# The end of a diffusion layer's expert stage: where the last down weights are loaded, where the first result tiles get their roots, which engine adds two of them

## The reference

```python
def ec_moe(h, router_w, w_gate, w_up, w_down):
    ...
    gate, idx = lax.top_k(jnp.swapaxes(aff, 1, 2), cap)      # 128 of 1024 tokens for each expert
    xs = h[bidx, idx]
    hid = jax.nn.silu(jnp.einsum("becd,edf->becf", xs, w_gate)) * jnp.einsum("becd,edf->becf", xs, w_up)
    ye = jnp.einsum("becf,efd->becd", hid, w_down) * gate[..., None].astype(h.dtype)
    return jnp.zeros_like(h).at[bidx, idx].add(ye)
...
y_lat = ec_moe(h_lat, router_w[l], exp_w_gate[l], exp_w_up[l], exp_w_down[l])
x = x + mod_lat[5] * rms_norm(y_lat, norm_g[l, 3])
```

## Time and profile before

| what | us |
|---|---|
| device time, median of three runs (1355.75 to 1360.29) | 1359.91 |
| the profiled execution: span from its first to its last instruction | 1356.6 |
| TensorE busy in that span | 1233.9 |
| VectorE busy | 765.7 |
| ScalarE busy | 429.7 |
| GpSimd busy | 225.3 |

### The profile page before, as it was taken

How to read it: one execution, slowest core, us unless ns; L and a number is a source line. 1 busy time by engine, 2 the same in 40 slices (tenths; PEclk the granted TensorE clock), 3 DMA queues, 4 the chain that set the end, 5 groups by cost and what they waited for, 6 DMA issues and landing times.

```text
span 1356.6 us, 14715 instructions
## 1 busy us (share of the span) xinstructions
PE 1233.9 (91%) x5488; PEld 717.2 (53%) x5488; DVE 765.7 (56%) x1113; ACT 429.7 (32%) x1109; POOL 225.3 (17%) x204
## 2 busy tenths in 40 slices
PE   5999999999989999899999779991599999999992
PEld 3555555455445555689999534441344444444441
DVE  5299889887925888389898457647500101010106
ACT  6333242313111112578877335531011010101113
POOL 0300000010000021266667000000101111010112
PEclk9999999999999999899999989995699999999996
DMA  9923444552142433466766735527389999999967
GB/s 364 282 78 111 130 151 139 147 164 85 45 145 58 88 80 82 106 197 208 231 221 193 279 139 187 186 78 287 116 309 330 338 334 339 338 329 343 323 223 198
DMA packets 206164, 270.69 MB, mean 200 GB/s; under 512 B 73685, under 2 KB 122830, under 8 KB 206094
## 3 DMA queue, kind: packets, MB, share of 16 engines
q1 hardware_dynamic: 186182, 212.54, 48.0%
q0 software_dynamic: 13840, 50.86, 12.2%
q10 hardware_dynamic: 6072, 6.35, 1.4%
HBM read 217.75 MB, written 51.97 MB: 199 GB/s over the span
## 4 chain that ended last, share of the span: by engine, by line
PE 78%; DVE 11%; DMA 5%; SPq 2%; ACT 2%; issue 1%; POOLq 0%; ACTq 0%; DVEq 0%
PE ps L2007 23%; PE ps L1193 16%; PE ps L1216 8%; PE ps L1150 8%; PE ps L448 5%; PE ps L429 4%; DMA arena<-ada_w 2%; DVE arena L2445 2%; DVE arena L2374 2%; DVE arena L2443 2%; DMA arena<-w_in 1%; PE ps L1906 1%; PE ps L522 1%; PE ps L495 1%; DMA scan_dram<-arena 1%
## 5 line engine op out<-in xcount | busy, mean ns | idle before, releaser
L2007 PE MATMUL ps<-arena 128*128 128x512 f32 (+1 forms) x1072 | 425.2, 555 | 5.1 <-DMA arena<-w_in 5.1
L2007 PEld LDWEIGHTS ps<-arena 128*128 128x128 f32 x1072 | 202.2, 191 | 205.5 <-issue 195.2
L1193 PE MATMUL ps<-arena 128*128 128x512 f32 x512 | 226.9, 597 | 1.4 <-ACT arena L1338 1.4
L2374 DVE SCALAR_TENSOR_TENSOR arena<-arena,taps 128x1024 f32<-128x1024 f32 x160 | 207.3, 1296 | 5.5
L1193 PEld LDWEIGHTS ps<-arena 128*128 128x128 f32 x512 | 96.7, 192 | 116.6 <-issue 114.8
L1525 DVE TENSOR_TENSOR arena<-arena,ps 128x512 f32<-128x512 f32 x16 | 11.0, 687 | 223.2 <-PE ps L1193 223.2
L1150 PE MATMUL ps<-arena 128*128 128x512 f32 x256 | 116.7, 604 | 1.3 <-DMA arena<-w_out 1.3
L1216 PE MATMUL ps<-arena 128*128 128x512 f32 x256 | 112.5, 593 | 0.0
L448 PE MATMUL ps<-arena 128*128 128x128 f32 (+5 forms) x632 | 72.6, 261 | 6.8 <-DVE arena L658 3.9
L1216 PEld LDWEIGHTS ps<-arena 128*128 128x128 f32 x256 | 47.6, 191 | 54.0 <-issue 54.0
L1150 PEld LDWEIGHTS ps<-arena 128*128 128x128 f32 x256 | 47.4, 193 | 52.3 <-issue 50.8
(11 more groups left out here) (332 smaller groups left out, 1577.0 us busy)
## 6 DMA issues: line engine op xcount, KB each, us to landing
arena<-exp_w_gate SPq DMA_DIRECT2D x16, 2048.0 KB, 11.0
arena<-exp_w_up SPq DMA_DIRECT2D x16, 2048.0 KB, 9.7
arena<-exp_w_down SPq DMA_DIRECT2D x16, 2048.0 KB, 10.9
arena<-ada_w POOLq DMA_DIRECT2D x16, 1024.0 KB, 6.5
arena<-w_in SPq DMA_DIRECT2D x28, 512.0 KB, 4.9
arena<-ada_w SPq DMA_DIRECT2D x4, 2048.0 KB, 19.7
arena<-x SPq DMA_DIRECT2D x16, 512.0 KB, 6.4
arena<-g_dram SPq DMA_DIRECT2D x16, 512.0 KB, 5.6
```

The costliest lines, as they stand in the source:

```text
L1193: last = mm(ps[gu_bank[s] + j][:], xsT[s][:, k, :], ew[s][j][:, k, :], start=(k == 0), stop=(k == KD - 1))
L2007: last = mm(ps[3 * (m % 2) + gi][:, 0:w], wring[(m + 1) % NW][:, k, :], hT[:, k, o:o + w], start=(k == 0), stop=(k == KD - 1))
L2374: ins = v.scalar_tensor_tensor(accg, cin_l[ci % 2][:, j // 3:j // 3 + GR, j % 3:j % 3 + GW], tp[:, j:j + 1], accg, ALU.mult, ALU.add)
```

## The change

Six edits, all in the end. The numbers in brackets are lines of the changed kernel where they differ.

1. SP: `load_down` of expert 15 is no longer issued in the experts' loop, but behind the first four of the eight loads of `yt`, ahead of the other four.
2. ScalarE: the roots of tiles 0 and 1 stand ahead of the last `hidT` copy, those of tiles 2 and 3 ahead of expert 14's `ye` copy; the two row roots come last, behind those of all tiles. RANK is gone, since the roots now run in the order of their numbers.
3. N_ACC is 6: tiles 0 to 5 are stored with an addition by GpSimd's transfers, tiles 6 and 7 plainly.
4. For tiles 6 and 7 the addition of `x2` is GpSimd's (a `tensor_tensor` of 128x1024, then its own plain store), no longer VectorE's with a store by SP.
5. VectorE scales tiles 0 to 5 ahead of the addition of `ye` to expert 14's rows, then tiles 6 and 7, then finishes expert 14's rows (`row_done(0)`).
6. VectorE's work on expert 15's rows, from the down product on, comes behind all that, and `row_done(1)` is last.

```diff
--- before.py
+++ after.py
@@ -984,8 +984,7 @@
         assert NL * D == 2 * KD * F and EL % 2 == 0
         x2r, yr = (xs[EL % NX - 2], xs[EL % NX - 1]), (xs[EL % NX], xs[EL % NX + 1])
         assert NX == 4 and EL % NX == 2
-        N_ACC = 5
-        RANK = [0, 1, 2, 3, NL] + list(range(4, NL)) + [NL + 1]
+        N_ACC = 6
 
         wo_k = w_out.rearrange("a (k p) n -> (a p) k n", p=P)
         wg_e = exp_w_gate.rearrange("a e (k p) n -> (a e) p k n", p=P)
@@ -1065,16 +1064,14 @@
                     sp_.wait_ge(sem("y_zero"), 32 * NL)
                 if e + 1 < E_N:
                     load_in(e + 1)
-                load_down(e)
+                if e < E_N - 1:
+                    load_down(e)
             sp_.wait_ge(sem("y_sc"), 16 * EL)
             sp_.wait_ge(sem("gu"), 2 * EL + 2)
             for t in range(NL):
+                if t == NL // 2:
+                    load_down(E_N - 1)
                 sp_.dma_start(yt[:, t, :], y_t[t]).then_inc(sem(f"tile_in{t // 2}"), 16)
-            for i in range(LE):
-                sp_.wait_ge(sem(f"xs_in{i}"), 16 * (E_N // NX + 1))
-            for t in range(N_ACC, NL):
-                sp_.wait_ge(sem("fin"), t + 1)
-                sp_.dma_start(out_t[t], yt[:, t, :]).then_inc(sem("out_full"), 16)
             sp_.wait_ge(sem("out"), 16 * N_ACC)
             sp_.wait_ge(sem("out_full"), 16 * (NL - N_ACC))
             sp_.wait_ge(sem("out_rows"), 16 * LE)
@@ -1339,9 +1336,8 @@
 
             def root_of(i, src):
 
-                n = RANK.index(i)
                 a(sqj, src, ACT.Square, accum_out=ssq[:, i:i + 1]).then_inc(sem("ysq"), 1)
-                act.wait_ge(sem("ysq"), 2 * n + 1)
+                act.wait_ge(sem("ysq"), 2 * i + 1)
                 a(rstd[:, i:i + 1], ssq[:, i:i + 1], ACT.Sqrt, scale=1.0 / D, bias=eps1[:]).then_inc(sem("ysq"), 1)
 
             def tile_root(t):
@@ -1356,13 +1352,16 @@
                     a(hid[e % 2], ps[gu_bank[e % 2]][:], ACT.Silu).then_inc(sem("sg"), 1)
                 if e + 1 < E_N:
                     xs_copy(e + 1, 0)
+                if e == E_N:
+                    tile_root(0)
+                    tile_root(1)
                 if e >= 1:
                     act.wait_ge(sem("hidps"), e)
                     a(hidT[(e - 1) % 2], heads(ps[1][:]), ACT.Copy).then_inc(sem("hidT"), 1)
                 if e + 1 < E_N:
                     xs_copy(e + 1, 1)
-            tile_root(0)
-            tile_root(1)
+            tile_root(2)
+            tile_root(3)
             act.wait_ge(sem("down"), EL + 1)
             act.wait_ge(sem("y_sc"), 16 * (EL - 1))
             for h in range(2):
@@ -1372,12 +1371,10 @@
             def row_root(i):
                 act.wait_ge(sem("rows"), i + 1)
                 root_of(NL + i, yr[i])
-            tile_root(2)
-            tile_root(3)
-            row_root(0)
             for t in range(4, NL):
                 tile_root(t)
-            row_root(1)
+            for i in range(LE):
+                row_root(i)
 
         def dve_tail(dve, link):
             v = nc.vector
@@ -1510,7 +1507,7 @@
             v.tensor_tensor(gateT, va, vb, ALU.max).then_inc(sem("route"), 1)
             dve.wait_ge(sem("route"), 5)
             def scaled(i, src):
-                dve.wait_ge(sem("ysq"), 2 * RANK.index(i) + 2)
+                dve.wait_ge(sem("ysq"), 2 * i + 2)
                 link(v.reciprocal(rstd[:, i:i + 1], rstd[:, i:i + 1]))
                 return v.scalar_tensor_tensor(src, src, rstd[:, i:i + 1], row5, ALU.mult, ALU.mult)
 
@@ -1536,13 +1533,14 @@
                 dve.wait_ge(sem(f"xs_in{EL % NX - 2 + i}"), 16 * (E_N // NX + 1))
                 v.tensor_tensor(yr[i], yr[i], x2r[i], ALU.add).then_inc(sem("fin"), 1)
 
-            scaled(0, yt[:, 0, :]).then_inc(sem("fin"), 1)
-            scaled(1, yt[:, 1, :]).then_inc(sem("fin"), 1)
+            for t in range(N_ACC):
+                scaled(t, yt[:, t, :]).then_inc(sem("fin"), 1)
             dve.wait_ge(sem("ye"), EL + 1)
             dve.wait_ge(sem(f"xs_in{EL % NX}"), 16 * (E_N // NX + 1))
             v.tensor_tensor(yr[0], yr[0], ye[EL % 2], ALU.add).then_inc(sem("rows"), 1)
-            for t in range(2, N_ACC):
+            for t in range(N_ACC, NL):
                 scaled(t, yt[:, t, :]).then_inc(sem("fin"), 1)
+            row_done(0)
             dve.wait_ge(sem("down"), E_N)
             dve.wait_ge(sem(f"xs_in{EL % NX + 1}"), 16 * (E_N // NX + 1))
             for h in range(2):
@@ -1555,13 +1553,9 @@
                 hs_ = slice(h * 512, (h + 1) * 512)
                 ins = v.tensor_tensor(yr[1][:, hs_], yr[1][:, hs_], ps[4 + h][:], ALU.add)
             ins.then_inc(sem("rows"), 1)
-            for t in range(N_ACC, NL):
-                link(scaled(t, yt[:, t, :]))
-                v.tensor_tensor(yt[:, t, :], yt[:, t, :], x2[:, t, :], ALU.add).then_inc(sem("fin"), 1)
-            for i in range(LE):
-                row_done(i)
-
-        def pool_tail(pool):
+            row_done(1)
+
+        def pool_tail(pool, link):
             p = nc.gpsimd
             scan_over(pool)
             for t in range(NL):
@@ -1610,6 +1604,10 @@
                 pool.wait_ge(sem(f"xs_in{i}"), 16 * (E_N // NX + 1))
             for t in range(N_ACC):
                 added(t)
+            for t in range(N_ACC, NL):
+                pool.wait_ge(sem("fin"), t + 1)
+                link(p.tensor_tensor(yt[:, t, :], yt[:, t, :], x2[:, t, :], ALU.add))
+                pool.dma_start(out_t[t], yt[:, t, :]).then_inc(sem("out_full"), 16)
             pool.wait_ge(sem("out"), 16 * N_ACC)
             pool.wait_ge(sem("out_full"), 16 * (NL - N_ACC))
             for i in range(LE):
@@ -1838,7 +1836,7 @@
                             channel_multiplier=0).then_inc(sem("c1"), 1)
 
             pool_scan(pool)
-            pool_tail(pool)
+            pool_tail(pool, link)
 
 
         @block.tensor
```

## The result

The changed kernel takes 1368.87 us (median of six runs, 1364.98 to 1373.28) against 1360.1 us for the kernel before on the same chip: a ratio of 1.0064, 95% interval 1.0041 to 1.0086. That is 8.7 us slower, clear of noise (the interval begins at 0.4%; whether the loss passes the 0.5% by which the prediction told "slower" from "same", it leaves open). 1363.0 us and "same" were predicted; the time lies 0.4 us above the range.

What follows compares the result with a forecast made beforehand. VectorE's list and nearly saturated DMA were taken to bound the end. Later loads and the tail put the first row scatter at 1349 against 1345.95: +3.0 us, span 1359.6, plus 3.3, rounded to 1363.0 us; range 1357 to 1368.5.

Steps and rivals of the forecast that it cites:

- The signs that the prediction named: First tile load near 1308.5, TensorE idle 2 us, tiles 4 to 7 late, GpSimd additions 2.5 to 4.3 us, scatter at 1349.
- the three that would have refuted it: Loads over by 1330, the scatter landing at 1312, or VectorE's rows still releasing the first row scatter.
- The scatter: 14th scatter, with the down-weight load moved away: 5.7 us instead of 9.4, so all loads start 3.6 us earlier.
- Rival B: The scatter's 9.4 us are its own cost, so it gains nothing: +6.6 us, 1366.5 us; chance 0.16.
- The early roots cost nothing: ScalarE's roots of tiles 0 and 1 take 4.0 us, over at about 1317.3, before the last hidT copy at 1319.10.
- At half share: Loads beside adding stores run at 0.205 MB/us: 2.1 MB of tiles 4 to 7 take 10.2 us, tile 7 landing at 1334.6.
- the weights run at 0.41: After the first four tiles, expert 15's down weights load at 0.41 MB/us until the early stores' bytes begin near 1321.8.
- Rival A: Adding stores hide in the loads without stretching them: scatter 3.3 us earlier than before, 1356.6 us; chance 0.13.
- The tail: From tile 7's landing at 1334.6 through roots, scaling, GpSimd additions and last store to the first row scatter at 1349.
- Rival C: GpSimd and VectorE block each other: each addition takes 4.3 us, VectorE waits as long; +5.6 us, 1365.5 us; chance 0.16.
- Both covered: VectorE finishes expert 14's rows at about 1342 and expert 15's at 1349; the second scatter waits for the first, landing 1352.8.
- The 3.3 us from span to median: The runs' median lies 3.3 us above the profiled span; taken as constant, it turns span 1359.6 into 1362.9.

Runs made afterwards that it cites:

- the kernel with late stores: Changed kernel with GpSimd held until the last tile load has landed before its first adding store: 1365.54 us, ratio 1.0029.

## Why the prediction was wrong

The signs that the prediction named came in kind, in other sizes, and none of the three that would have refuted it: the path was right, and a rate on it was wrong.

**The scatter** was right: 5.9 us alone (5.7 taken), against 9.4 behind a load. Rival B, by which it would gain nothing, fell.

**The early roots cost nothing** was right for what the step looked at, ScalarE and the `hidT` copy; alone they indeed cost nothing. The step also named where the danger lay, the early start of four stores beside the loads.

**"At half share" is the step that failed.** "q1 has 2.1 MB of tiles 4 to 7 left at 1323.7, at 0.205 MB/us 10.2 us": the rate was 0.137. It entered twice, in the rest of the weights (0.38 MB) and in the four tiles. The tiles landed 31.5 us behind the scatter's landing instead of 26.1, 5.4 us more. The rate makes 4.4 of them: from the stores' first bytes, at 20.2 us, q1 had 2.45 MB left, as predicted within 0.03 MB, and took 16.5 us for them instead of 12.1 (at 0.137 all the way it would have been 17.9; the early stores ran out at 1341, and the last 0.3 MB ran alone). The other 1.0 us lies ahead of that, and is a smaller error of the same step: "the weights run at 0.41", but from 1321 to 1325 q1 alone, with full engines, moved 0.36 MB/us. The earlier trace rows had 0.33 for such a load (1.19 MB in 3.6 us), and the 0.98 MB that were taken for the 2.8 us ahead of the gathers are 0.35, not "slightly under 0.41". So the stores' bytes met the loads at 20.2 us and not at 19.1:

```profile
q1 hardware_dynamic: 348, 1.42, 97.8%
```

The weights landed 3.3 us later than predicted: 1.2 us by this later start, 0.6 by the rate. The other 1.5 us are open: by 1328.2 q1 had moved as many bytes as the first four tiles and the weights hold, but the weights landed at 1330.4. TensorE waited 5.4 us, near the bound of 5.6 that had been set for another reason, a scatter that lands at 9.4.

The rate came from one microsecond in which a load stood beside an addition, 53 packets against 25: a microsecond in which q0 had only begun. Two longer rows of before, both on record, would have given it. The gathers beside the loads show equal packets, 274 and 284. And a packet that adds costs 12 × 16 × 1.056 / 656 = 0.309 us of an engine, a loaded one 4 × 16 × 1.027 / 450 = 0.146. Turn by turn the sixteen engines then load 16 / 0.455 = 35 packets of 3.67 KB a microsecond, 0.129 MB. The Trainium skill ("DMA: Bandwidth & Descriptors", Queues, rings and completion order) says that an engine goes round-robin between queue rows and changes only at packet boundaries; the traces agree in all four cases (559 and 566, 554 and 567, 346 and 344, 274 and 284 packets). The prediction didn't use it.

**Rival A**, that the stores hide in the loads, was refuted by the same rows. Its price was gauged by how the loads fare, and they fared worse than in the forecast, not better.

**The tail** was a little better than predicted: 13.0 us from the last tile to the scatter against 14.4. A GpSimd addition takes 2.34 us (2.5 taken). Rival C is half right: VectorE does wait for most of GpSimd's addition, 2.12 us twice, but GpSimd's own 2.34 us are below its low bound. In the kernel with late stores GpSimd's first addition took 3.96 us and the scaling beside it 5.03, the size that rival C assumed.

**"Both covered" was wrong for the second scatter.** VectorE was done with expert 15's rows at 1360.9, 1.9 us after the first scatter had landed (1355.67 + 3.34). From the last tile to expert 14's rows it took 11.3 us instead of 7.4; without the two waits of 2.12 us it would have been 7.1. Expert 15's rows took the 6.9 us that were foreseen. The two scatters lie 5.5 us apart instead of 4.6: 0.9 us more.

The sum, behind S: 5.5 us for the tiles (0.2 from the scatter, 1.0 ahead of the sharing, 4.4 from the rate, within rounding), −1.4 in the tail, +0.9 for the second scatter, +0.3 behind it make 5.3, the distance from 56.8 to 62.2 within rounding. The 3.3 us from span to median that were taken as constant aren't one: 1.7 to 1.8 of them lie between every run's time and its own span, the rest is that the profiled execution was faster than the median (in the changed kernel the median lies 1.4 above the span). Of the whole loss of 8.35 us by the trace, 5.75 come with edit 1 and the early roots of edit 2, almost all of it from their meeting. The other 2.6 come with the rest of edit 2 and edits 3 to 6; 1.9 us go when GpSimd's additions do, and how the rest is split was not measured.

## What to carry to other kernels

When two DMA queues run together, count packets: here they took turns, so each queue's rate on an engine was its packet's bytes over the sum of both packets' costs, and the cheap transfer pays for the dear one. An accumulating store that starts early isn't free work in an idle place if loads that gate the next stage are still out; edits that are harmless alone should be costed together where they share a queue. And an operation handed to another engine may cost the giver more than the operation did: here 2.12 us of waiting for 1.23 us of work.

## What the runs showed of the hardware

- An accumulating store beside loads holds 68.7% of the DMA engines and leaves the loads 0.137 MB/us of 0.41; a plain store leaves them 0.21.
- An accumulating scatter of 0.5 MB takes 5.9 us alone, 9.4 with a 2 MB load ahead of it. The Trainium skill ("DMA: Bandwidth & Descriptors", Anatomy of one DMA) gives fixed cost and rate from which 3.2 us had been estimated; the measurement differs, and decides. A plain scatter of as many rows took 3.34 us.
- A short idle time of TensorE can cost clock or not. After 1.84 us of idle 16 matmuls took 7.10 us, after 1.59 us 7.11; after 1.91 us they took 8.80, after 2.64 us 8.80 and after 5.38 us 9.04. So the 4 us of idle time that rival B took from the end of the kernel before is no bound for such a loss; why 1.91 us cost clock and 1.84 us didn't, no run here shows. In the run with 1.91 us (the changed kernel with late roots) the granted clock (the third column from the end, behind POOL's busy time) fell although TensorE was busy in all three stretches of 2 us:

```profile
1326.00:1328.00 2.00, 1.90 (x3) 0.91 (x4) 1.96 (x3) 1.94 (x6) 1.74 (x2) 0.67 1.03 414
1328.00:1330.00 2.00, 2.00 (x4) 0.72 (x3) 1.70 (x3) 2.00 (x4) 0.99 (x2) 0.50 1.02 354
1330.00:1332.00 2.00, 2.00 (x6) 0.97 (x5) 1.28 (x2) 1.93 (x6) 0.85 (x1) 0.98 1.06 225
```

  0.50 is 1.2 GHz, and it came back to 2.4 GHz while the matmuls ran on. The 1.7 us that it cost lay beside other work there: VectorE took that product last, at 1344.3, and TensorE was done by 1336.7.
